# A decoder step: its own buffer for the state-space convolutions, the conformer norm two tiles sooner, other shares of VectorE's work per tile

## The reference

```python
u = x @ w_in[l]
z, xbc, dt_raw, q, k, v, qi, ki, wi, glu = jnp.split(u, points, axis=-1)
xbc = silu(causal_dwconv(xbc, ssd_conv_prev, ssd_conv_w[l], ssd_conv_b[l]))   # 4 taps, 768 channels
y_ssd = rms_norm((ssd_scan(...) + d * xs) * silu(z), ssd_norm_g[l])
q, k, qi, ki = rope(q), rope(k), rope(qi), rope(ki)
y_att = attend(q, k, v, qi, ki, wi)     # index scores choose 256 keys for each query: lax.top_k
gl = glu[..., :256] * sigmoid(glu[..., 256:])
c = causal_dwconv(gl, cc_conv_prev, cc_conv_w[l], cc_conv_b[l])               # 31 taps, 256 channels
y_cc = silu(layer_norm(c, cc_ln_g[l], cc_ln_b[l]))
x = layer_norm(ALPHA * x + concat([y_ssd, y_att, y_cc]) @ w_out[l], ...)
...    # then a gated feed-forward part with a 3-tap convolution, and a norm
```

## Time and profile before

| | |
|---|---|
| time, three runs | 3828.7, 3820.38, 3825.1 us; median 3825.1 |
| profiled execution | 3816.51 us, of which the span is 3814.7 us |
| granted TensorE clock, mean | 0.919 |
| busy share of the span: PE, DVE, ACT, POOL | 87%, 50%, 32%, 17% |
| the stage in layer 0 | 203.90 to 588.20 us |

### The profile page before, as it was taken

The page is one execution under the profiler, slowest core; times in us unless marked ns, Lnnn a source line. Parts: engine busy times, 40 slices in busy tenths (PEclk is TensorE's granted clock), DMA queues, the critical chain, the costliest instruction groups (busy, mean ns, idle before and its releaser), DMA issues.

```text
span 3814.7 us, 51646 instructions
## 1 busy us (share of the span) xinstructions
PE 3304.1 (87%) x19286; PEld 2652.2 (70%) x19286; DVE 1909.9 (50%) x2976; ACT 1236.7 (32%) x2251; POOL 638.6 (17%) x651
## 2 busy tenths in 40 slices
PE   4899887857889999999868998786669999999995
PEld 2454455624789999999834453564349899999994
DVE  4467864332475434334435868633226645335335
ACT  3246623333252112212223574243333412112213
POOL 0000000001013333333100000000110333334331
PEclk8999998857999999999989998897589999999998
DMA  3111104304301111111021110142151111111111
GB/s 100 49 36 29 32 17 124 94 17 123 102 17 35 52 48 37 53 50 34 27 81 48 34 34 23 62 117 63 35 155 40 34 45 36 54 45 37 55 34 58
DMA packets 169894, 206.59 MB, mean 54 GB/s; under 512 B 61025, under 2 KB 138146, under 8 KB 168738
## 3 DMA queue, kind: packets, MB, share of 16 engines
q1 hardware_dynamic: 143138, 185.36, 16.4%
q10 hardware_dynamic: 26496, 17.84, 1.6%
HBM read 187.17 MB, written 15.96 MB: 53 GB/s over the span
## 4 chain that ended last, share of the span: by engine, by line
PE 64%; DVE 16%; ACT 9%; SPq 5%; issue 3%; DMA 2%; POOL 0%; ACTq 0%; DVEq 0%; POOLq 0%
PE PS L742 41%; PE PS L723 7%; DVE WORK L1668 4%; DVE MIX L1668 2%; ACT WORK L1435 2%; PE PS L755 2%; PE PS L827 2%; ACT X L1306 2%; SPq L424 2%; SPq L425 2%; DVE WORK L1860 1%; PE PS L935 1%; DMA RING<-cache_k 1%; PE PS L781 1%; DVE WORK L1632 1%
## 5 line engine op out<-in xcount | busy, mean ns | idle before, releaser
L742 PE MATMUL PS<-WORK_parts,WHIGH_parts 128*128 128x352 f32 x4224 | 869.5, 328 | 35.2 <-POOL WORK_parts L709 17.7
L723 PE MATMUL PS<-X,RING 128*128 128x512 f32 (+1 forms) x2016 | 671.8, 496 | 109.3 <-DMA RING<-w_in 65.4
L742 PEld LDWEIGHTS PS<-WORK_parts,WHIGH_parts 128*128 128x128 f32 x4224 | 724.2, 191 | 38.9 <-issue 20.6
L742 PE MATMUL PS<-WORK_parts,RING_parts 128*128 128x352 f32 x3168 | 691.3, 327 | 0.0
L723 PEld LDWEIGHTS PS<-X,RING 128*128 128x128 f32 x2016 | 338.4, 194 | 443.8 <-issue 375.2
L742 PEld LDWEIGHTS PS<-WORK_parts,RING_parts 128*128 128x128 f32 x3168 | 545.4, 190 | 0.0
L1668 DVE SCALAR_TENSOR_TENSOR WORK<-WORK,VEC 128x1072 f32<-128x1072 f32 (+2 forms) x272 | 525.6, 1932 | 9.7
L1252 ACT ACTIVATE WORK<-PS 128x32 f32<-128x32 f32 (+11 forms) x412 | 190.8, 514 | 842.1 <-PE PS L742 579.7
L489 POOL TENSOR_TENSOR RING_parts<-RING,WHIGH_parts 128x1024 fp32r<-128x1024 f32 (+2 forms) x184 | 372.0, 2022 | 467.2 <-ACT WHIGH_parts L1252 466.9
L742 PE MATMUL PS<-X_parts,WHIGH_parts 128*128 128x352 f32 x2016 | 434.4, 323 | 0.0
L1435 ACT ACTIVATE WORK<-WORK 128x512 bf16<-128x512 f32 x310 | 285.7, 922 | 198.5 <-DVE WORK L1907 198.4
(11 more groups left out here) (318 smaller groups left out, 3722.2 us busy)
## 6 DMA issues: line engine op xcount, KB each, us to landing
RING<-w_up SPq DMA_DIRECT2D x88, 512.0 KB, 3.6
RING<-cache_k SPq DMA_DIRECT2D x200, 128.0 KB, 2.2
RING<-cache_v SPq DMA_DIRECT2D x192, 128.0 KB, 2.1
RING<-w_in SPq DMA_DIRECT2D x46, 512.0 KB, 3.6
RING<-w_down SPq DMA_DIRECT2D x80, 256.0 KB, 2.7
RING<-cache_v ACTq DMA_DIRECT2D x64, 128.0 KB, 2.5
RING<-cache_k ACTq DMA_DIRECT2D x56, 128.0 KB, 2.6
yT<-X SPq DMA_DIRECT2D x5, 1408.0 KB, 5.5
```

The lines of the kernel that those rows point to most:

```text
L723: mm = pe.matmul(job_psum(n, w, first=first), stationary(k), moving(k)[:, first:first + w], start=k == 0, stop=k == k_tiles - 1)
L742: mm = pe.matmul(thirds(n)[:, third, :], a, x[:, third * THIRD:(third + 1) * THIRD], start=k == 0 and part == 0, stop=k == tiles - 1 and p ...
```

## The change

The state-space convolution gets a place of its own, SSD_ACC in MIX[:, 2:4], which z2 and z3 fill later. With that the second conformer half no longer waits for the sixth state-space convolution, and the marks for it go. The mean stands in JOBS before q0 instead of v0, the variance before q1 instead of v1. And the row of numbers that VectorE spends at the end of a tile is another: 2 instead of 4 in the xbc tiles; 0 instead of 4 in the gate, glu and z tiles; 0 for k0 and 5 for k1 as before; 8 instead of 11 for q0 and q1; 6 for v0 and v1 as before. ScalarE's sixth silu (behind z0's copy) and its copy of z2 into MIX[:, 2] stand in that order on one engine.

```diff
@@ JOBS, the list of projections and small products @@
-    if _j == T_V:
+    if _j == T_Q:
         JOBS.append(("mean", "cc"))
-    if _j == T_V + 1:
+    if _j == T_Q + 1:
         JOBS.append(("var", "cc"))
@@ the views on the on-chip memory @@
+        SSD_ACC = MIX[:, 2:4, :].rearrange("p a b -> p (a b)")[:, 0:SSD_LEN]
         ACC = [MIX[:, 4:6, :].rearrange("p a b -> p (a b)")[:, 0:CC_LEN], view(CC_LEN)]
@@ ScalarE, silu_xbc @@
-                    act.activation(XBC[:, t, 0:SEQ], ACC[1][:, 0:SEQ], ACT.Silu, bias=v(V_SSDB + t))
+                    act.activation(XBC[:, t, 0:SEQ], SSD_ACC[:, 0:SEQ], ACT.Silu, bias=v(V_SSDB + t))
...
@@ VectorE, convolve_conformer @@
                     for t in range(2):
-                        while t and not ssd_convolved:
-                            yield 1.0
-                        if t:
-                            dve.wait_ge(silu_done, 6)
                         await_freed(dve, JOB[("in", T_GLU + t)])
@@ VectorE, project, a state-space tile @@
-                        inline.append(convolve_by_taps(ACC[1][:, 0:SSD_LEN - SSD_H], XBC[:, t, :], SSD_W,
+                        inline.append(convolve_by_taps(SSD_ACC[:, 0:SSD_LEN - SSD_H], XBC[:, t, :], SSD_W,
@@ VectorE, the loop over the stage's jobs @@
                         search(j)
-                        if j == T_Z:
-                            ssd_convolved.append(True)
                         if j == LAST_BITS:
                             aside.append(chosen)
-                        spend(4 if j < T_K else 0 if j == T_K else 5 if j < T_Q else 11 if j < T_V else 6, aside)
+                        spend(2 if j < T_GATE else 0 if j <= T_K else 5 if j < T_Q else 8 if j < T_V else 6, aside)
```

## The result

The changed kernel takes 3785.5 us (median of four runs, 3781.48 to 3793.96) against 3822.7 us before: a ratio of 0.9905 (95% interval 0.9882 to 0.9927). 37 us are gained; 33.5 were forecast. Its profiled execution took 3781.48 us, 35.0 us less than that of before.

What follows compares the result with a forecast made beforehand. The stage was taken as bound by its search chain, TensorE carried along. Each layer gains 16.8 us before B and loses 0.1 in the tail; doubled, 33.5 off the 3825.1 median gives 3791.5, range 3776 to 3812.

Steps and rivals of the forecast that it cites:

- Bound: Stage's search: 31 steps, each needing the step before, with ScalarE's scan and VectorE's counting; TensorE is carried along.
- Gate, convolution and z tiles: Stretches before the last three steps: gate and glu gain 14.5 us, convolution loses 22.4, z gains 24.7.
- The five-tap step: Second step of a convolution tile, holding five conformer taps: 3.08 + 8.00 = 11.08 us by the formula.
- B: End of the last search step, the start of L1913 at 488.39; to come 16.8 us sooner in a layer.
- the meeting of the chains: At k1's end: its product copied at 466.9, the last step wanted at 466.4 plus 0.4; they arrive together.
- The first rival: TensorE takes over the chain, gaps costing 2.5 us in k0, k1 and 1.9 in q1: 3805.3 us; chance 0.14.
- the four new gaps: TensorE gaps ahead of z1, z3, the mean and q0; by the skill's clock rule each new gap starts slow.
- The tail: From B to the stage's end: B + 97.9 us now, B + 98.0 after, a loss of 0.1 a layer.
- Doubling: Layer 1's stage runs like layer 0's, so the layer sum is doubled: 33.5 us.
- The moved norm: Mean before q0, variance before q1: q0 starts 14.8 us later relative to B, given back by v1's end.
- the cheap case: Convolution steps stay at 7.94 us with all taps in the wait; gain 38, but TensorE caps B at 30 sooner.

Runs made afterwards that it cites:

- even taps: Changed kernel with 1 instead of 2 spent behind a convolution tile and 2 instead of 3 in each step from z0 on; 3759.1 us.
- the shared accumulator: Changed kernel with the shared accumulator ACC[1] and its wait for ssd_convolved put back, new row and early norm kept; 3790.3 us.
- even taps and the other tail: Changed kernel with 1 behind a convolution tile, 2 per step from z0, and 16, 14, 6, 0 behind q0, q1, v0, v1; 3754.1 us.

## Why the prediction was right

**Bound.** Right. What ties the stage together is a chain of 31 steps, and a step is as long as the longer of two things: ScalarE's scan, with the copy and the silu that stand ahead of it, or what VectorE was given to do in it. TensorE enters where that copy waits for its product, as with the buffer alone. The steps' lengths in layer 0, from one L1906 (L1903 after) of VectorE to the next:

| us | glu0, gate1, glu1 | convolution tiles, second steps | z0, z1 | z2, z3 | k0 and k1 |
|---|---|---|---|---|---|
| before | 8.9, 12.7, 7.9, 13.9, 8.0, 12.7 | 9.3, 8.0, 8.0, 8.0, 8.0, 5.6 | 6.8, 8.8, 7.9, 12.7 | 7.9, 12.7, 7.9, 12.5 | 5.6, 5.6, 5.2 |
| after | 8.9, 7.9, 7.9, 9.1, 8.0, 7.9 | 11.1, 11.1, 13.5, 11.1, 11.1, 11.1 | 7.9, 7.9, 7.9, 6.1 | 5.6, 5.6, 5.6, 5.6 | 5.6, 5.6, 6.0 |

**Gate, convolution and z tiles.** Forecast -14.5, +22.4 and -24.7; measured -14.4, +22.2 and -24.9. The five-tap step, the one price that no row showed, took 11.07; 11.08 was taken from the formula, with 7.94 and 12.68 as its ends. In the steps in which it doesn't wait, VectorE's time here is the sum of its instructions.

**B.** Forecast 16.8 sooner. Measured 16.3 in layer 0 and 17.1 in layer 1. The 0.5 of layer 0 is the meeting of the chains: the last step waits 3.39 instead of 2.60, since k1's projection, which ran on from z3's cold start at 416.14, came that much late for ScalarE; in layer 1 the same three projections took 48.41 instead of 49.63, and the last step waits 2.60. The first rival named that place and put 6.9 us on it; 0.8 in one layer is what there was. Its cold starts in k0, k1 and q1 did not come: these ran in 15.68 or joined without a gap. Of the four new gaps that the prediction listed, those ahead of z1, z3 and the mean were followed by a slow start, the one ahead of q0 (0.81) was not. That TensorE came only 0.8 late is in part luck, since the two chains were forecast within 0.1 of each other; with the buffer alone it came 7.7 late.

**The tail.** Forecast 0.1 longer, measured 1.4 shorter in layer 0 (2.1 in layer 1). The mis-sized term is q0: it was priced at 17.3 from a cold start, and ran 15.68, behind a mean product that ran slow instead (7.05, where 3.9 was set). The mean was no part of the path to q0, which waits for VectorE's rotation. That is 1.6, and accounts for layer 0. It is luck, not foresight: with the shared accumulator, in the same order of jobs, q0 ran 17.37. In layer 1 the tail of before was 0.7 longer still (q0 17.94, v1 17.95 there), which the doubled sum left out. The rest of that chain came as written: q0 at B + 10.3 (10.2), v1 without a wait.

**Doubling.** 17.8 and 19.2; forecast 16.7 each.

**What it did not see.** The moved norm was booked as neutral, by the balance of one timing. The runs show that it is worth 1 to 2 us a layer beside the old row and 3.4 to 4.5 beside the new one, for there the v1 wait of 7.71 would have grown to 10.85, by the tie set that 8 instead of 11 leaves behind v0's copy. The prediction said that the wait must go, but not what the row would have made of it if the norm had stayed. And the limit put on the cheap case, B no more than 30 us sooner because of TensorE's projections, was the more useful number: with even taps B came 29.0 sooner than before.

## What to carry to other kernels

Where a chain of equal steps hides other work, write down each step's length with its filling and compare it with the length unfilled: work beyond the wait costs its full time, and an unfilled wait is lost, so the filling wants to be even over the steps (four and two taps here, not five and none). An edit that is nearly neutral beside the old order of the other work, as the norm and the buffer here, can count beside the new one, so weigh it together with the rest of the change. When a tail is shortened, look at once for what ends just before the thing that was last, on every queue, stores that only a stage's end waits for among them.

## What the hardware showed that I had not expected

The slow start behind a gap can fall on a short product. A mean product that took 4.07 warm took 7.05 after 6.29 us of idling, and the full projection that followed, after another 0.81, ran at 15.68: the slow start fell on a short product that is off the path, and the long one behind it had none. The same place shows it with the old row (5.79 and 15.68) and with even taps and the other tail (6.57 and 15.68). But it can't be relied on. Mean and q0 with the norm alone, against the rows shown for the shared accumulator:

```profile
490.17 5.60 PE L723 MATMUL PS<-MIX,MEAN 128*128 128x512 f32 x12 [21.26 <-ACT MIX L1359]
...
498.04 15.68 PE L723 MATMUL PS<-X,RING 128*128 128x512 f32 x48 [2.26 <-DVE WORK L1686]
```

With the norm alone q0 ran at full rate behind gaps of 21.26 and 2.26 us; with the shared accumulator, behind 20.82 and 2.00, both were slow, 6.77 and 17.37, and layer 1 repeats either outcome. Nor does a gap by itself tell if a product starts slow. The fourth convolution tile's projection came behind a gap of 2.29 us before and of 2.30 with the buffer alone (layer 0): it took 15.68, at a granted clock of 1.00 from its start, and 18.75, at 0.50 in its first 3.3 us. What decides between the two these runs don't show.
